# One decoder layer on one core: a ring of six places inside the expert loop, a reordered last pair of experts, and a reordered start

## What is computed

```python
def moe_ffn(x, w_router, b_router, w_gate_up, b_gate_up, w_down, b_down):
    logits = (xt @ w_router + b_router).astype(jnp.float32)
    top_val, top_idx = lax.top_k(logits, TOP_K)             # 4 of 32 experts
    gates = jax.nn.softmax(top_val, axis=-1)
    ...
    def expert_block(args):
        xb, e = args
        h = xb @ w_gate_up[e] + b_gate_up[e]                # 1024 -> 2048
        g, u = h[:, :D_EXPERT], h[:, D_EXPERT:]
        g = jnp.minimum(g, SWIGLU_LIMIT)
        u = jnp.clip(u, -SWIGLU_LIMIT, SWIGLU_LIMIT)
        glu = g * jax.nn.sigmoid(g * SWIGLU_ALPHA)
        return ((u + 1.0) * glu) @ w_down[e] + b_down[e]    # 1024 -> 1024
```

## Time and profile before

| | us |
|---|---|
| median of 3 runs | 1226.02 (1224.87 to 1226.47) |
| the profiled execution | 1225.65 |
| its span | 1223.8 |
| PE busy | 1152.3 (94%) |
| DMA queue q1, share of 16 engines | 86.6% |
| first gate matmul of the experts | 291.47 |
| first gate matmul of the last pair | 1154.31 |

### The profile page before, as it was taken

How to read it: one execution, slowest core, us unless ns; L and a number is a source line. 1 busy time by engine, 2 the same in 40 slices (tenths; PEclk the granted TensorE clock), 3 DMA queues, 4 the chain that set the end, 5 groups by cost and what they waited for, 6 DMA issues and landing times.

```text
span 1223.8 us, 13031 instructions
## 1 busy us (share of the span) xinstructions
PE 1152.3 (94%) x5372; PEld 523.7 (43%) x5372; DVE 219.8 (18%) x552; ACT 133.9 (11%) x288; POOL 48.6 (4%) x59
## 2 busy tenths in 40 slices
PE   9999999999999999999899999898989789998985
PEld 7686746754334343433333443333333324342421
DVE  1223112124211111121111211111111111111113
ACT  2133101221000000000000100000000000000002
POOL 0032003210000000000000000000000000000000
PEclk9999999999999999999999999999999989999999
DMA  9943333386999999999999999999999999999993
GB/s 357 314 157 138 125 122 140 130 341 242 428 415 427 428 428 429 428 427 427 428 427 427 428 427 429 428 428 426 428 428 427 427 427 427 428 428 428 428 428 121
DMA packets 54391, 445.93 MB, mean 364 GB/s; under 512 B 10136, under 2 KB 11296, under 8 KB 29760
## 3 DMA queue, kind: packets, MB, share of 16 engines
q1 hardware_dynamic: 52032, 439.96, 86.6%
q10 hardware_dynamic: 2304, 5.12, 1.2%
HBM read 444.01 MB, written 1.06 MB: 364 GB/s over the span
## 4 chain that ended last, share of the span: by engine, by line
PE 67%; DMA 28%; DVE 2%; issue 2%; ACT 1%; POOL 0%; SPq 0%; DVEq 0%
PE bank L1527 21%; DMA ring<-in_w_gate_up 18%; PE bank L1548 13%; DMA reg_kv<-in_w_gate_up 9%; PE bank L1187 9%; PE bank L1174 9%; PE bank L1426 5%; PE bank L1487 2%; PE bank L1502 2%; PE bank L1537 1%; PE bank L1371 1%; PE bank L1205 1%; DMA ring<-in_w_in 1%; DVE reg_k L1085 1%; DVE reg_k L1082 0%
## 5 line engine op out<-in xcount | busy, mean ns | idle before, releaser
L1527 PE MATMUL bank<-ring,PT 128*64 128x512 f32 x1392 | 309.7, 596 | 25.9 <-DMA ring<-in_w_gate_up 18.2
L1527 PEld LDWEIGHTS bank<-ring,PT 128*64 128x64 f32 x1392 | 98.3, 137 | 231.9 <-issue 194.3
L1548 PE MATMUL bank<-ring,NCt 128*64 128x512 f32 x672 | 148.8, 595 | 0.7 <-ACT NCt L717 0.7
L1174 PE MATMUL bank<-reg_bc,ring 128*128 128x256 f32 x480 | 106.7, 381 | 1.8 <-ACT reg_bc L642 1.8
L1077 DVE TENSOR_SCALAR reg_k<-bank 128x512 f32<-128x512 f32 x32 | 22.1, 692 | 465.9 <-PE bank L1527 465.9
L708 ACT ACTIVATE reg_v<-reg_k 128x512 f32<-128x512 f32 x32 | 20.2, 630 | 744.4 <-DVE reg_k L1077 744.4
L1174 PEld LDWEIGHTS bank<-reg_bc,ring 128*128 128x128 f32 x480 | 90.3, 190 | 16.6 <-issue 4.8
L1548 PEld LDWEIGHTS bank<-ring,NCt 128*64 128x64 f32 x672 | 46.4, 137 | 100.0 <-issue 91.5
L1527 PE MATMUL bank<-reg_kv,PT 128*64 128x512 f32 x336 | 75.9, 594 | 5.7 <-DMA reg_kv<-in_w_gate_up 5.7
L1094 DVE COPY reg_v<-bank 128x512 f32<-128x512 f32 x32 | 22.1, 692 | 304.3 <-PE bank L1548 304.3
L1426 PEld LDWEIGHTS bank<-L,reg_a 128*128 128x128 f32 x512 | 62.9, 196 | 24.8 <-issue 23.5
(11 more groups left out here) (215 smaller groups left out, 681.3 us busy)
## 6 DMA issues: line engine op xcount, KB each, us to landing
ring<-in_w_gate_up SPq DMA_DIRECT2D x87, 2048.0 KB, 34.7
ring<-in_w_down SPq DMA_DIRECT2D x42, 2048.0 KB, 38.3
reg_kv<-in_w_gate_up SPq DMA_DIRECT2D x21, 2048.0 KB, 36.8
reg_q<-in_w_down SPq DMA_DIRECT2D x11, 2048.0 KB, 35.2
reg_bc<-in_w_down SPq DMA_DIRECT2D x11, 2048.0 KB, 36.6
reg_q<-in_w_gate_up SPq DMA_DIRECT2D x10, 2048.0 KB, 31.7
reg_bc<-in_w_gate_up SPq DMA_DIRECT2D x10, 2048.0 KB, 33.2
ring<-in_w_in SPq DMA_DIRECT2D x5, 2048.0 KB, 17.5
```

Source lines behind the costliest of these rows:

```text
L1174: last = mm(B(name)[:, a * T:(a + 1) * T], w[:, k, c:c + P], src[:, k, :], start=(k == 0), stop=(k == KD - 1))
L1527: last = mm(ps[half * CAP:(half + 1) * CAP, :], xgT[:, k, i * CAP:(i + 1) * CAP], w[:, j, col:col + HALF], start=False, stop=(k == KD - 1) ...
L1548: last = mm(xy_ps[half * CAP:(half + 1) * CAP, :], hT[:, a:a + CAP], w[:, j, half * HALF:(half + 1) * HALF], start=(k == 0), stop=(k == KD ...
```

## The change

- **Start.** The identity is issued ahead of the tokens on SP; each half of the tokens has a semaphore of its own, and PE turns all blocks of the second half (ACT's queue) first, then of the first. The first weight group comes in pieces of 512 KB, 512 KB and 1 MB. The first projection makes all 512 columns in one pass over the rows.
- **Places.** The first 36 chunks (three pairs) use the nine places as before. From pair 3 to 14, chunk c of every expert goes to place c, so a loop over single pairs does for PE (pairs 3 to 5, pair 6 alone, pairs 7 to 14), and a loop over single experts for SP.
- **Last pair.** Its twelve chunks go over all nine places (`FINAL`) and are issued in the order gate chunks of 30, gate chunks of 31, down chunks of 30, down chunks of 31, the last of them in three pieces (`PIECES`). PE's `final_pair` makes both `gate_up` before the two down products, the second product in another bank (`tr_ps`), with the hidden rows of expert 31 in another tile (`hT_last`). The turning of expert 31's hidden rows stands in the middle of expert 30's down product; the scatter of expert 30 is cut in halves, one ahead of expert 31's down product and one behind. DVE's program follows: two activations, then two copies.

The semaphores `x_in`, `first_in`, `piece_in` become lists, `scatter` takes a list of token tiles, DVE's activation is a function `swiglu` with the instructions of before, and ACT copies into `hT_last` for the last expert. The core of the diff:

```diff
@@ -72,6 +72,13 @@
 ORDER = [4, 0, 1, 5, 6, 7, 8, 2, 3]
 NSLOT = len(ORDER)
+OPEN = 2 * NSLOT // CH
+RINGED = OPEN * 2 * CH // NSLOT - OPEN * 2
+
+
+FINAL = {(0, 0): 0, (0, 1): 1, (0, 2): 2, (0, 3): 3, (1, 0): 6, (1, 1): 7, (1, 2): 8, (1, 3): 4,
+         (0, 4): 5, (0, 5): 0, (1, 4): 1, (1, 5): 2}
+PIECES = [(0, 2), (2, 3), (3, 4)]
 def t5_bucket(n):
@@ -416,12 +425,11 @@
             def load_small(g):
                 if g == "qf":
-                    sp.dma_start(x_nat[:, 0, :], x[0, 0:P, :]).then_inc(x_in, 16)
                     sp.dma_start(K[:, 0:P], consts[:, 0:P]).then_inc(ident_in, 16)
+                    sp.dma_start(x_nat[:, 0, :], x[0, 0:P, :]).then_inc(x_in[0], 16)
                     w = group_source(g)
-                    for k in range(0, KD, 4):
-                        sp.dma_start(group_tile(g)[:, k:k + 4, :], w[:, k:k + 4, :]).then_inc(
-                            first_half_in if k == 0 else group_in[0], 16)
+                    for k0, k1, arrived in ((0, 2, first_in[0]), (2, 4, first_in[1]), (4, KD, group_in[0])):
+                        sp.dma_start(group_tile(g)[:, k0:k1, :], w[:, k0:k1, :]).then_inc(arrived, 16)
                     sp.wait_ge(wf_zeroed, 1)
                     sp.dma_start(wf[:, :, 0:NFOX], w_in[0][:, 3 * FW:3 * FW + NFOX].rearrange("(k p) n -> p k n", p=P)).then_inc(wf_in, 16)
                     sp.dma_start(bf[:, :], b_forget[0].rearrange("(h o) -> h o", o=1)).then_inc(wf_in, 16)
@@ -465,20 +473,34 @@
                     wait_filled(sp, ("co" if slot == GSLOTS + 2 else "cqk", NCH - 1))
                 load_chunk(n // CH, n % CH, n)
-            def reload(e, u, c):
-
-                wait_used((c + 3) % CH, e - 1 if c < 3 else e)
-                load_chunk(e, c, u * CH + c)
-
-            for n in range(NSLOT, 3 * CH):
-                reload(n // CH, n // CH, n % CH)
-            with sp.Fori(1, NE // 3) as t:
-                for u in range(3):
-                    for c in range(CH):
-                        reload(t * 3 + u, u, c)
-            for e in range(NE // 3 * 3, NE):
+            for n in range(NSLOT, OPEN * 2 * CH):
+                wait_used((n - NSLOT) % CH, (n - NSLOT) // CH + 1)
+                load_chunk(n // CH, n % CH, n)
+            for c in range(CH):
+                n = OPEN * 2 * CH - NSLOT + c
+                wait_used(n % CH, n // CH + 1)
+                load_chunk(OPEN * 2, c, c)
+            with sp.Fori(OPEN * 2 + 1, NE - 2) as e:
                 for c in range(CH):
-                    reload(e, e % 3, c)
+                    wait_used(c, e)
+                    load_chunk(e, c, c)
+            for c in range(GUC):
+                wait_used(c, NE - 2)
+                load_chunk(NE - 2, c, FINAL[0, c])
+            for c in range(GUC - 1):
+                load_chunk(NE - 1, c, FINAL[1, c])
+            wait_used(4, NE - 2)
+            load_chunk(NE - 1, 3, FINAL[1, 3])
+            wait_used(5, NE - 2)
+            load_chunk(NE - 2, 4, FINAL[0, 4])
+            wait_used(0, NE - 1)
+            load_chunk(NE - 2, 5, FINAL[0, 5])
+            wait_used(1, NE - 1)
+            load_chunk(NE - 1, 4, FINAL[1, 4])
+            wait_used(2, NE - 1)
+            n, e, c = FINAL[1, 5], NE - 1, CH - 1
+            for piece, (j0, j1) in zip(piece_in, PIECES):
+                sp.dma_start(slot_tile(n, c)[:, j0:j1, :], chunk_source(e, c)[:, j0:j1, :]).then_inc(piece, 16)
             sp.wait_ge(tables_ready, 1)
             pairs = sp.value_load(ctl[0:1, MAXX:MAXX + 1], min_val=0, max_val=MAXX // 2)
@@ -1096,8 +1123,16 @@
             with dve.Fori(0, BASE_PAIR) as p:
                 pair(p)
             pair(BASE_PAIR, with_base=True)
-            with dve.Fori(BASE_PAIR + 1, NE // 2) as p:
+            with dve.Fori(BASE_PAIR + 1, NE // 2 - 1) as p:
                 pair(p)
+            p = NE // 2 - 1
+            for i in range(2):
+                swiglu(p, i)
+            places(S, p + 1, False).then_inc(s_ready, 1)
+            places(Sg, p + 1, True).then_inc(sg_ready, 1)
+            for i, ps in enumerate((xy_ps, tr_ps)):
+                dve.wait_ge(y_done, p * 2 + i + 1)
+                nc.vector.tensor_copy(ysb[:, i, :], ps[:, :]).then_inc(y_sb, 1)
             extra = dve.value_load(ctl[0:1, MAXX:MAXX + 1], min_val=0, max_val=MAXX // 2)
             with dve.If(extra > 0):
                 with dve.Fori(NE // 2, extra + NE // 2) as p:
@@ -1156,9 +1191,16 @@
             for _ in range(3):
                 mm(bank[7][:, 0:3 * P], c8[:, 0:P], c8[:, :], start=True, stop=True)
             pe.wait_ge(ident_in, 16)
-            pe.wait_ge(x_in, 16 * TT)
-            for j in range(4):
-                transposes(x_nat, "xT", j)
+            for tt in (1, 0):
+                pe.wait_ge(x_in[tt], 16)
+                for j in range(4):
+                    name = ("xT", j)
+                    for a in range(2):
+                        k = 2 * j + a
+                        last = nc.tensor.transpose(B(name)[:, a * T + tt * P:a * T + (tt + 1) * P],
+                                                   x_nat[:, tt, k * P:(k + 1) * P], ident)
+                    if tt == 0:
+                        fill(last, name)
             def columns_out(g, j, src, arrived=None):
@@ -1193,19 +1235,22 @@
             def x_arrived(k):
                 if k % 2 == 0:
                     wait_evacuated(pe, ("xT", k // 2))
-                if k == 0:
-                    pe.wait_ge(first_half_in, 16)
+                if k in (0, 2):
+                    pe.wait_ge(first_in[k // 2], 16)
                 elif k == 4:
                     wait_group(pe, "qf")
-            name = ("qf", 0)
+            for j in range(2):
+                wait_bank(pe, ("qf", j))
             for k in range(KD):
                 x_arrived(k)
-                for a in range(2):
-                    last = mm(B(name)[:, a * T:(a + 1) * T], group_tile("qf")[:, k, a * P:(a + 1) * P], reg_b[:, k, :],
-                              start=(k == 0 and a == 0), stop=(k == KD - 1), skip_group_check=True)
-            fill(last, name)
-            columns_out("qf", 1, reg_b)
+                for j in range(2):
+                    for a in range(2):
+                        c = (2 * j + a) * P
+                        last = mm(B(("qf", j))[:, a * T:(a + 1) * T], group_tile("qf")[:, k, c:c + P], reg_b[:, k, :],
+                                  start=(k == 0 and a == 0), stop=(k == KD - 1), skip_group_check=True)
+                    if k == KD - 1:
+                        fill(last, ("qf", j))
             pe.wait_ge(wf_in, 32)
             name = ("fpart", 0)
@@ -1501,17 +1546,24 @@
                     rows = slice(g * 2 * NE, (g + 1) * 2 * NE)
                     mm(ps[:, :], bsel[rows, i, :], bgu[rows, :], start=True, stop=False, skip_group_check=True)
-            def chunk(turn, u, i, c):
-
-                if u is None:
-                    loads = NE * CH // NSLOT + (c < NE * CH % NSLOT)
-                    pe.wait_ge(slot_in[c], turn * 32 + (i + 1 + loads - NE) * 16)
-                    return slot_tile(c, c)
-                m = (u * 2 + i) * CH + c
-                pe.wait_ge(slot_in[m % NSLOT], turn * 64 + (m // NSLOT + 1) * 16)
-                return slot_tile(m, c)
-
-            def gate_up(p, i, turn, u):
+            def chunk(p, i, c, stage):
+
+                if stage == "open":
+                    n = (p * 2 + i) * CH + c
+                    loads = n // NSLOT + 1
+                elif stage == "loop":
+                    n, loads = c, p * 2 + (i + 1 + RINGED)
+                elif stage == "final":
+                    n = FINAL[i, c]
+                    loads = OPEN * 2 * CH // NSLOT + 1
+                    if n < CH:
+                        loads += NE - 2 - OPEN * 2 + ((i, c) in ((0, 5), (1, 4)))
+                else:
+                    n, loads = c, p * 2 + (i + 1 + RINGED + (1 if c < 2 else 0) - 1)
+                pe.wait_ge(slot_in[n % NSLOT], loads * 16)
+                return slot_tile(n, c)
+
+            def gate_up(p, i, stage):
                 if i == 0:
                     pe.wait_ge(xgTa_sb, p + 1)
@@ -1552,9 +1604,56 @@
                 if k == KD - 1:
                     last.then_inc(y_done, 1)
-            def pair(p, turn, u, first=False, with_base=False, last=False):
-
-                gate_up(p, 0, turn, u)
+            def final_down(p, i, ps, h, between=None):
+
+                for k in range(KD):
+                    c, j = GUC + k // DNJ, k % DNJ
+                    if (i, c) != (1, CH - 1):
+                        if j == 0:
+                            w = chunk(p, i, c, "final")
+                    else:
+                        w = slot_tile(FINAL[i, c], c)
+                        for piece, (j0, _) in zip(piece_in, PIECES):
+                            if j == j0:
+                                pe.wait_ge(piece, 16)
+                    a = (k % 4) * P + (k // 4) * CAP
```

(78 more changed lines are left out.)

49 lines of the change are left out of this document (27 added, 22 removed).

## The result

The changed kernel takes 1219.32 us, the median of five runs (1218.44 to 1220.11); the kernel before took 1226.02 beside it. The ratio is 0.9947, with a 95% interval of 0.9935 to 0.9959: faster by 6.7 us, more than the 2.45 that can be told. The forecast was 1218.5. The profiled execution took 1219.3 us, with a span of 1217.4 against 1223.8, so the 6.4 us between the spans are what has to be found.

What follows compares the result with a forecast made beforehand. The weight stream's start and rate, and PE's work after the last landing, were taken to set the end. From the profiled 1225.65 us, 1225.65 - 0.7 - 4.6 - 1.8 = 1218.5, with a range from 1215.5 to 1229.

Steps and rivals of the forecast that it cites:

- What bounds it: Whole kernel: the end is set by the weight stream's start, its rate, and PE's work after the last landing.
- Part 1: Start: the smaller first piece lets the projection begin at 7.95 instead of 8.65; -0.7 us, between 0.1 and 0.9 gained.
- Part 2: Six ring places from pair 3 to 14: the stream does not run dry; cost 0, bound +2 us.
- Part 3: One-pair loops: code stays held, nine jumps cost 50 ns each, three stream losses fewer; -4.6 us, bounds 0 and -6.
- rival A: Pair loops: each of nine jumps back costs 9.47 us like the old one, end near 1260; chance 0.10.
- Part 4: Last pair: reordered work starts the last scatter at 1209.6 against 1211.42; -1.8 us, bounds -2.7 and -0.5.
- B: Pair loops: jumps miss but hide in PE's slack, two stream losses more from extra fetches, 1226.2 us; chance 0.20.
- C: Stream: fetches have nothing to do with the losses, or the thinner queue gives as much back, 1223 us; chance 0.10.
- D: Last pair: gains nothing because pieces of 4 KB rows land late, 1220 us; chance 0.60 together with the forecast.
- The signs: Trace: 25 to 27 fetches, 50 ns branches, 58.7 us pairs, no 0.50 clock, projection at 7.9 to 8.0, scatter 7 us sooner.

Runs made afterwards that it cites:

- written out: Changed kernel with both of TensorE's pair loops replaced by straight code, no jump back: 1222.58 us, ratio 0.9969 to the kernel before.
- four pairs: Changed kernel with TensorE's second loop given a body of four pairs, two passes, 2,124 instructions: 1221.85 us, ratio 0.9963 to the kernel before.
- moved by 40: Changed kernel with three pairs a pass in TensorE's second loop and ten single-column warm-up matmuls shifting the code 40 instructions: 1225.18 us, ratio 0.9993 to before.
- the kernel before moved: Kernel before with one single-column matmul added among the warm-up matmuls, shifting its code by four instructions: 1225.17 us, ratio 0.9995 to the kernel before.
- the two kernels with 34 fetches: Changed kernel with three pairs a pass in TensorE's second loop, 1220.30 us; the same with code shifted four instructions, 1219.82 us.
- the early jump: Changed kernel with the jump over unused code put ahead of expert 30's down product, the last down products written twice: 1222.77 us, ratio 0.9968 to before.
- the whole last chunk: Changed kernel with the last chunk loaded in one 2 MB piece instead of three: 1219.48 us, ratio 0.9940 to the kernel before.

## Why the prediction held

**What bounds it.** Right: the stream of weights sets the end, before as after, with 37 waits for chunks from 380 us on and pairs of 58.7 to 58.8.

**Part 1, -0.7.** -0.24 in the profiled run, -0.8 in the one with short transposes (first expert 290.67 against 291.47), -0.5 to -0.9 over all. The step was right but for one premise: that 2.14 us of transposes is a constant. It was one value out of a spread from 1.91 to 3.00, set for the most part by when TensorE's clock rises.

**Part 2, 0.** Right. Ring loads land 24.0 us after issue at the median, and where the queue is thinnest, at 458, 11.3 us after (I had worked out about 10); the rate stays at 426 to 430. In stream against fetches the kernels with nine places (913.0 for 48, 911.7 for 39) lie in one row with those with six (912.2 for 45, 912.0 for 43), so no price of the six places shows. Six places from the first pair on show the other side of it: 14 us.

**Part 3, -4.6.** -4.1. Both halves of the step held: nine jumps of about 210 ns (I had said 50; nothing hangs on it), and a loss of some 1.5 us with every eighth fetch, 14 fetches in the stream against 35. In place of three losses fewer, the runs give a price for each fetch: 22 fetches between the two kernels (21 of them in the stream) for 4.0 us of stream, 19 for 3.2 (written out), 17 for 3.0 (four pairs), 18 for 4.0 (moved by 40), 9 for 1.3 (the kernel before moved): 0.14 to 0.22 us each. It is a mean, and one execution can be a loss off: the two kernels with 34 fetches lie 1.6 and 0.9 above the changed one (0.20 and 0.11 for each of eight), the old last pair, with 26, 0.7 under it, and the early jump and the whole last chunk, with its 26 fetches, 1.1 and 1.6, though each of these changed something at the end too. That the old stall came from the end of a block, my argument against rival A, is borne out by the stalls of 2.36, of 1.95 and 3.43, and of 7.70 at three places of the head, one execution each. One reading was loose: eight fetches for the second pass over some 1,590 instructions make one for 200; the figure of about 260 is that of the first pass, with six fetches from 798.3 to 939.2.

**Part 4, -1.8.** -2.07, and the old last pair put back costs 1.9 by the medians and 1.4 by the landings. The first half of the last scatter ends 13.7 us behind the tenth landing, where the prediction had 13.4, and the gap around the jump was 0.92 us instead of the 1.54 that it took over from the kernel before: 0.3 more and 0.6 less, which is why the step gave 0.3 more than forecast.

**The rivals.** A and B fall with the branches of 213 and 208 ns and the 26 fetches; the four pairs a pass show what B would have looked like, 43 fetches and 2.5 us lost. C falls with the written-out loops. D falls with the 2.07 us and the old last pair put back; its late pieces are not there: nothing waits for them, and they are worth nothing either. (In A's sum, nine jumps of 9.47 put the start of the last pair at 1195.8, not 1195.1; nothing changes by it.) The Trainium skill ("Runtime: NRT & Kernel Launch", Instruction fetch mechanics) has a taken branch out of a window of two pages wait for a fetch. The runs here say otherwise for TensorE: a jump back over seven blocks took 220 ns. Its 2,048 instructions for TensorE, eight blocks, agree with what stayed and what did not.

**The signs.** The fetches (26), the pairs of 58.7 and the rate came as said. Four did not, to the letter. The branches last 208 to 213 ns at the median, not some 50. The projection starts at 8.37 in the profiled run, not at 7.9 to 8.0, and the last scatter comes 6.4 us sooner, not 7. And the granted clock is once 0.50 in the stream, from 307.8 to 311.2, after PE had stood still for 2.42 us; it was paid out of the surplus of the nine places: the profiled run with the old start has no such stretch and took 1219.47 against 1219.30.

The forecast lies 0.8 us under the median: against the profiled run 0.5 is the start, 0.5 the stream, and the last pair gives 0.3 back.

## What to carry to other kernels

Where a stream of weights sets the end, count the code as part of it: each block of instructions fetched during the stream cost 0.11 to 0.22 us here, so loops small enough to stay pay even if no jump ever stalls. Before blaming the length of a loop, count the blocks it touches and where its head and its branch lie; four instructions decided between 249 and 6375 ns. And buffers that matter while a stream fills may be given up once it is bound: look at the two phases separately.

## What the runs showed beyond that

- Held code behaved as eight blocks of 256 instructions, with the next one asked for only after a block is entered; a jump from the third instruction of a block still came ahead of it.
- A jump that misses lasts 6.0 to 6.4 us while the weights stream, 7.7 in one case near the end of the stream, and 3.3 to 3.9 when the stream is over (4.7 and 4.9 in the two kernels with the old program); what PE loses of it went from 2.36 to 7.70 us, by the place of the head in its block.
- The losses of the stream come whole (6.45 between landings instead of 4.89) in the kernel before, in two parts (5.46 and 5.85) in the written-out one, and in four or more of 5.1 to 5.5 with four pairs a pass. But the pattern comes back every eight fetches in all of these: with four pairs a pass the landings take 5.35, 5.48, 5.18 and 5.07 around the fetches 19, 20, 23 and 24 of the page, and nearly the same again around 27, 28, 31 and 32, which is 1.5 us over 4.89 for eight fetches, or 0.19 for each. Why it is cut up in such ways wasn't tried.
- TensorE's clock rose at 5.1 to 7.7 us in twelve of the thirteen profiled executions, after warm-up matmuls that began at 1.50 in all; transposes come 0.21 us apart before that and 0.11 behind it. A granted clock of 1.00 printed for the first microseconds of a kernel is no evidence, since the trace has no record there; the spacing of equal matmuls is.
